# The first block's convolved projection with seven products of quarter sums, the weight sums made on GpSimd

## What is computed

```python
proj = h @ w_in[layer]                      # (256, 1024) @ (1024, 9304)
(..., qkv_b, ...) = jnp.split(proj, IN_SPLIT_IDX, axis=-1)     # qkv_b: 3072 columns
qkv_b = jax.nn.silu(causal_depthwise_conv(qkv_b, conv_w[layer]))   # 4 taps over the tokens
q_b, k_b, v_b = jnp.split(qkv_b, [1024, 2048], axis=-1)
q_b = l2_normalize(q_b.reshape(B, S, 8, 128))
k_b = l2_normalize(k_b.reshape(B, S, 8, 128))
```

## Time and profile before

| | us |
|---|---|
| median of 3 runs | 2429.8 (2429.56 to 2431.7) |
| the profiled execution's own time | 2429.32 |
| its span | 2427.4 |
| TensorE busy | 2369.2 (98%) |
| VectorE busy | 764.1 (31%) |
| ScalarE busy | 462.0 (19%) |
| GpSimd busy | 136.4 (6%) |
| mean granted TensorE clock | 0.992 of full speed |

### The profile page before, as it was taken

One profiled execution on the slowest core, in us unless ns is written; L12 is line 12 of the kernel. 1 busy time (PEld: TensorE's weight loads), 2 busy tenths in 40 slices (PEclk: granted clock), 3 DMA queues, 4 the chain that ended last, 5 costly groups with the idle time before them and its releaser, 6 DMA issues. The chain is left out here.

```text
span 2427.4 us, 51178 instructions
## 1 busy us (share of the span) xinstructions
PE 2369.2 (98%) x23267; PEld 1376.0 (57%) x23267; DVE 764.1 (31%) x1542; ACT 462.0 (19%) x793; POOL 136.4 (6%) x355
## 2 busy tenths in 40 slices
PE   9999999999999989999999899999999999999999
PEld 8755557856555666997455655435343534443444
DVE  3544623445633554663024532101010101101012
ACT  1531321432323542000015431000000000000001
POOL 4011000011000310000003100000000000000000
PEclk9999999999999999999999999999999999999999
DMA  7522334432335413445447128999999999999992
GB/s 244 166 88 72 120 122 139 145 105 71 108 116 142 158 54 126 166 162 177 142 129 192 55 91 330 397 405 373 384 391 383 372 395 396 398 378 392 389 370 97
DMA packets 194445, 542.54 MB, mean 224 GB/s; under 512 B 29200, under 2 KB 61360, under 8 KB 194224
## 3 DMA queue, kind: packets, MB, share of 16 engines
q1 hardware_dynamic: 180576, 536.82, 60.5%
q10 hardware_dynamic: 13344, 1.35, 0.4%
q0 software_dynamic: 304, 1.05, 0.1%
HBM read 538.12 MB, written 1.05 MB: 222 GB/s over the span
## 5 line engine op out<-in xcount | busy, mean ns | idle before, releaser
L405 PE MATMUL psum<-ring,hT 128*128 128x512 f32 (+3 forms) x1120 | 477.1, 575 | 6.1 <-ACT area L829 4.5
L2877 PE MATMUL psum<-ring,mix 128*32 128x448 f32 x4608 | 438.7, 539 | 0.2 <-DVE mix L3139 0.2
L405 PEld LDWEIGHTS psum<-ring,hT 128*128 128x128 f32 x1120 | 206.1, 190 | 206.1 <-issue 180.8
L2877 PEld LDWEIGHTS psum<-ring,mix 128*32 128x32 f32 x4608 | 149.1, 110 | 282.4 <-issue 280.6
L3128 DVE TENSOR_TENSOR area<-area,psum 128x1344 f32<-128x1344 f32 x16 | 24.6, 1535 | 457.6 <-PE psum L2877 457.6
L710 PE MATMUL psum<-hT,ring 128*128 128x256 f32 x768 | 166.4, 379 | 0.0
L710 PEld LDWEIGHTS psum<-hT,ring 128*128 128x128 f32 x768 | 146.1, 190 | 20.5 <-issue 1.0
L2890 PE MATMUL psum<-area 128*32 128x256 f32 x2688 | 148.2, 379 | 0.9 <-DVE area L3130 0.9
L2877 PE MATMUL psum<-area,mix 128*32 128x448 f32 x1536 | 147.3, 539 | 0.0
L2890 PE MATMUL psum<-ring,area 128*32 128x256 f32 x2688 | 146.5, 379 | 0.0
L2890 PEld LDWEIGHTS psum<-area 128*32 128x32 f32 x2688 | 86.7, 110 | 60.5 <-issue 2.9
(11 more groups left out here) (559 smaller groups left out, 2507.2 us busy)
## 6 DMA issues: line engine op xcount, KB each, us to landing
ring<-in_w_in_dram SPq DMA_DIRECT2D x88, 1024.0 KB, 5.1
ring<-in_moe_w_gate_dram SPq DMA_DIRECT2D x96, 896.0 KB, 7.0
ring<-in_moe_w_up_dram SPq DMA_DIRECT2D x96, 896.0 KB, 7.6
area<-in_moe_w_down_dram SPq DMA_DIRECT2D x112, 512.0 KB, 5.9
ring<-in_moe_w_down_dram SPq DMA_DIRECT2D x112, 512.0 KB, 6.3
area<-in_moe_w_gate_dram SPq DMA_DIRECT2D x32, 896.0 KB, 7.4
area<-in_moe_w_up_dram SPq DMA_DIRECT2D x32, 896.0 KB, 7.3
ring<-in_w_out_dram SPq DMA_DIRECT2D x16, 1024.0 KB, 5.1
```

The costliest lines, as they stand in the source:

```text
L405: last = nc.tensor.matmul(acc(g)[:, t, 0:d["n"]], lhs(kk, t), w[:, k, :], start=kk == 0, stop=kk == d["nk"] - 1)
L2877: last = nc.tensor.matmul(PS[32 * j:32 * j + 32, 3 * p + b, 0:PIECE].rearrange("p (m n) -> p m n", n=32), tokens(k, b), w[:, :, j, :], sta ...
```

## The change

Tile 0 stays as it was. Tiles 1 to 5 of each layer are computed by the seven-product form of Strassen and Winograd on one level: the weights are cut into four quarters (512 input rows by 256 columns), the input into four (512 channels by 128 tokens), and seven products of sums of quarters take the place of eight. A product is 8 matmuls of 128x128.

- `quarter_sums`: for each tile GpSimd makes four sums of 128x1024 from the tile's weights in the ring; all operands lie in SBUF. Two sets of buffers take turns, so the sums of tile i wait for the sixth product of tile i-2.
- `qkv_token_sums`: VectorE makes four sums of 128x512 of the input once per layer, behind the norm.
- `qkv_seven`: TensorE's products go round the four banks 0 to 3. The second product of a tile waits for GpSimd's sums; the fifth for ScalarE's copy of the first (`QKEPT`); the sixth and seventh for VectorE's reads of the second and third.
- `qkv_quarters`: VectorE joins the products by seven additions of 128x256, each with one input in PSUM and one in SBUF. They stand in VectorE's program ahead of the tile's convolution, and for tile 4 of the first layer ahead of the set-up.
- `proj1_act`: for tiles 1 to 5 ScalarE copies only the first product.
- Some semaphores are renamed into chains, so that there are enough of them.

```diff
+        def quarter_sums(s, eng, g, sums, name):
+            lo, hi = quarter_operands(g)
+            s1, s2, s3, s4 = sums
+            s.do(eng.tensor_tensor(s1, lo[:, :, IN1], hi[:, :, IN1], ALU.add))
+            s.do(eng.tensor_tensor(s2, s1, lo[:, :, IN0], ALU.subtract))
+            s.do(eng.tensor_tensor(s3, lo[:, :, IN0], lo[:, :, IN1], ALU.subtract))
+            s.after(eng.tensor_tensor(s4, hi[:, :, IN0], s2, ALU.subtract).then_inc(sem(name), 1), name)
+        def quarter_product(out, w, h):
+            for j in range(2):
+                for k in range(4):
+                    last = nc.tensor.matmul(out[:, j, :], w[:, k, j * P:(j + 1) * P], h[:, k, :], start=k == 0, stop=k == 3)
+            return last
+        def qkv_bank(i, place):
+            return PS[:, (2 + 7 * (i - 1) + place) % 4, 0:256].rearrange("p (j s) -> p j s", j=2)
+        def qkv_seven(pe, L, i):
...
+            order = ((lo[:, :, IN0], HT[:, 0:4, TOK0]), (s2, t2), (s1, t1), (s3, t3), (hi[:, :, IN0], HT[:, 4:8, TOK0]),
+                     (s4, HT[:, 4:8, TOK1]), (hi[:, :, IN1], t4))
+            gemm_begin(pe, g)
+            for h in range(2):
+                landed(pe, d["first"] + h)
+            for place, (w, h) in enumerate(order):
+                if place == 1:
+                    pe.wait_ge(sem("qkv_sums"), 5 * L + i)
+                if place == 2 and i == 1:
+                    pe.wait_ge(sem("gemm_out_act"), evacuated(group("qkv", L)[0])[1])
+                if place < 4:
+                    pe.wait_ge(sem("qkv_by_vector"), qkv_read(L, i - 1, 3 + place) if i > 1 else 31 * L + 1)
+                elif place == 4:
+                    pe.wait_ge(sem("gemm_out_act"), evacuated(g)[1])
+                else:
+                    pe.wait_ge(sem("qkv_by_vector"), qkv_read(L, i, place - 4))
+                quarter_product(qkv_bank(i, place), w, h).then_inc(sem("weights_used" if place > 4 else "qkv_product"), 1)
+        def qkv_pool(s, L):
+            if L:
+                x_half(s.eng, L, 1)
+            else:
+                s.eng.wait_ge(sem("param_cols_T"), 1)
+            for i in range(1, 6):
+                gs = group("qkv", L)
+                if i > 2:
+                    s.eng.wait_ge(sem("weights_used"), used(TILES[gs[i - 2]]["first"]))
+                for h in range(2):
+                    landed(s.eng, TILES[gs[i]]["first"] + h)
+                quarter_sums(s, nc.gpsimd, gs[i], QSUM[i % 2], "qkv_sums")
+        def qkv_token_sums(s):
+            t1, t2, t3, t4 = QTOK
+            s.do(nc.vector.tensor_tensor(t1, HT[:, 0:4, TOK1], HT[:, 0:4, TOK0], ALU.subtract))
...
+        def qkv_quarters(s, L, i):
...
+            first = 25 * L + 5 * (i - 1)
+            s.eng.wait_ge(sem("gemm_out_act"), evacuated(g)[1])
+            s.eng.wait_ge(sem("qkv_product"), first + 2)
+            told_read(add(QBOTH, qkv_bank(i, 1), QKEPT, ALU.add))
+            s.eng.wait_ge(sem("qkv_product"), first + 3)
+            told_read(add(QTHREE, qkv_bank(i, 2), QBOTH, ALU.add))
...
             for j, g in enumerate(group("qkv", L)):
-                s.eng.wait_ge(sem("weights_used"), used(TILES[g]["end"] - 1))
-                src = acc(g).rearrange("p b (j s) -> p (b j) s", j=2)
-                s.after(nc.scalar.activation(XC[:, 4 * j:4 * j + 4, 3:3 + S], src, ACT.Copy).then_inc(sem("gemm_out_act"), 1), "gemm_out_act")
+                if j:
+                    s.eng.wait_ge(sem("qkv_product"), 25 * L + 5 * (j - 1) + 1)
+                    if j > 1:
+                        s.eng.wait_ge(sem("qkv_by_vector"), qkv_read(L, j - 1, 4))
+                    dst, src = QKEPT, qkv_bank(j, 0)
...
+            qkv_token_sums(s)
             s.do(nc.vector.memset(XC[:, :, 0:3], 0.0))
...
             for j, g in enumerate(group("qkv", L)):
+                if j:
+                    qkv_quarters(s, L, j)
                 if L == 0 and j == 4:
                     setup_dve(s)
                     trig_tables(s, None)
...
             for L in range(DEPTH):
+                qkv_pool(s, L)
                 gdn_pool(s, L)
```

More of the change, by code:

```diff
@@ L670, in blocks_kernel @@
         XC = view(14512, CT * (S + 3)).rearrange("p (c s) -> p c s", c=CT)
+        QSUM = [[view(a, 1024).rearrange("p (k c) -> p k c", k=4) for a in (0, 1024, 3144, 4168)],
+                [v.rearrange("p (k c) -> p k c", k=4)
+                 for v in (mix_t[:, 0:1024], mix_t[:, 1024:2048], view(6288, 1024), view(7328, 1024))]]
+        QTOK = [view(a, 512).rearrange("p (k s) -> p k s", k=4) for a in (20728, 21240, 21752, 2048)]
+        QKEPT, QBOTH, QTHREE = [view(a, 256).rearrange("p (j s) -> p j s", j=2) for a in (22264, 5192, 5448)]
@@ new lines, in blocks_kernel, with quarter_operands @@
+        IN0, IN1, TOK0, TOK1 = slice(0, 256), slice(256, 512), slice(0, P), slice(P, S)
+        def quarter_operands(g):
+            return [half_view(TILES[g]["first"] + h, (4, 512)) for h in range(2)]
+        def quarter_sums(s, eng, g, sums, name):
[5 more added lines that the diff above has]
+            s.after(eng.tensor_tensor(s4, hi[:, :, IN0], s2, ALU.subtract).then_inc(sem(name), 1), name)
@@ new lines, in qkv_token_sums, with told_read @@
+        def qkv_token_sums(s):
+            t1, t2, t3, t4 = QTOK
+            s.do(nc.vector.tensor_tensor(t1, HT[:, 0:4, TOK1], HT[:, 0:4, TOK0], ALU.subtract))
+            s.do(nc.vector.tensor_tensor(t2, HT[:, 4:8, TOK1], t1, ALU.subtract))
+            s.do(nc.vector.tensor_tensor(t3, HT[:, 4:8, TOK1], HT[:, 0:4, TOK1], ALU.subtract))
+            s.after(nc.vector.tensor_tensor(t4, HT[:, 4:8, TOK0], t2, ALU.subtract).then_inc(sem("qkv_by_vector"), 1), "qkv_by_vector")
+        def qkv_quarters(s, L, i):
+            g = group("qkv", L)[i]
+            out = XC[:, 4 * i:4 * i + 4, 3:3 + S]
+            add = nc.vector.tensor_tensor
+            def told_read(ins):
+                s.after(ins.then_inc(sem("qkv_by_vector"), 1), "qkv_by_vector")
+            first = 25 * L + 5 * (i - 1)
[4 more added lines that the diff above has]
+            told_read(add(QTHREE, qkv_bank(i, 2), QBOTH, ALU.add))
+            s.eng.wait_ge(sem("qkv_product"), first + 4)
+            s.do(add(QBOTH, qkv_bank(i, 3), QBOTH, ALU.add))
+            told_read(add(out[:, 2:4, TOK1], qkv_bank(i, 3), QTHREE, ALU.add))
+            s.eng.wait_ge(sem("qkv_product"), first + 5)
+            told_read(add(out[:, 0:2, TOK0], qkv_bank(i, 4), QKEPT, ALU.add))
+            s.eng.wait_ge(sem("weights_used"), used(TILES[g]["first"]))
+            told_read(add(out[:, 0:2, TOK1], qkv_bank(i, 5), QTHREE, ALU.add))
+            s.eng.wait_ge(sem("weights_used"), used(TILES[g]["end"] - 1))
+            told_read(add(out[:, 2:4, TOK0], qkv_bank(i, 6), QBOTH, ALU.add))
@@ L700, in proj1_pe @@
             for i, g in enumerate(group("qkv", L)):
+                if i:
+                    qkv_seven(pe, L, i)
+                    if i == 3:
+                        sums(0)
+                    continue
                 d = TILES[g]
@@ L715, in proj1_pe @@
                             last.then_inc(sem("weights_used"), 1)
-                if i == 3:
-                    sums(0)
+            pe.wait_ge(sem("qkv_by_vector"), qkv_read(L, 5, 6))
             for _ in range(8):
@@ L766, in proj1_act @@
             for j, g in enumerate(group("qkv", L)):
-                s.eng.wait_ge(sem("weights_used"), used(TILES[g]["end"] - 1))
-                src = acc(g).rearrange("p b (j s) -> p (b j) s", j=2)
-                s.after(nc.scalar.activation(XC[:, 4 * j:4 * j + 4, 3:3 + S], src, ACT.Copy).then_inc(sem("gemm_out_act"), 1), "gemm_out_act")
+                if j:
[3 more added lines that the diff above has]
+                    dst, src = QKEPT, qkv_bank(j, 0)
+                else:
+                    s.eng.wait_ge(sem("weights_used"), used(TILES[g]["end"] - 1))
+                    dst, src = XC[:, 0:4, 3:3 + S], acc(g).rearrange("p b (j s) -> p (b j) s", j=2)
+                s.after(nc.scalar.activation(dst, src, ACT.Copy).then_inc(sem("gemm_out_act"), 1), "gemm_out_act")
                 if L == 0 and j < 4:
@@ L1371, in trig_tables @@
                     s.do(nc.vector.tensor_scalar(dst, dst, 3.1415925, -3.1415925, ALU.min, ALU.max))
-                s.after(nc.vector.tensor_copy(POSF, POSF).then_inc(sem("angles"), 1), "angles")
+                s.after(nc.vector.tensor_copy(POSF, POSF).then_inc(signal("angles"), 1), "angles")
             else:
                 s = s_act
-                s.eng.wait_ge(sem("angles"), 1)
+                s.eng.wait_ge(signal("angles"), reached("angles", 1))
                 s.do(nc.scalar.activation(SIN, SIN, ACT.Sin))
@@ L3531, in _ @@
             n = at_n = 0
[L3532 removed]
+            pe.wait_ge(signal("ident_ready"), reached("ident_ready", 1))
             keep_busy(3, 4)
```

31 lines of the change are left out of this document (20 added, 11 removed).

## The result

| | us |
|---|---|
| changed kernel, median of 4 runs | 2504.34 (2500.51 to 2506.15) |
| the kernel before, median of 4 runs beside it | 2430.75 (2429.56 to 2434.91) |
| ratio | 1.0298, 95% interval 1.0279 to 1.0316 |
| the profiled execution's own time, and its span | 2500.51, 2498.6 |

The account below looks back on a forecast made before the run. TensorE, busy 98% of the span, was taken to bound the kernel. 2429.3 + 32.5 (first layer) + 19.8 (second layer) + 8 (clock) = 2489.6, so 2490 us, with a 0.8 range of 2443 to 2510.

Parts of the forecast that it names:

- The products' saving: Tiles 1 to 5, both layers: 12.51 us a tile instead of 13.86, 13.5 us saved over ten tiles if nothing waits.
- A sum of 2.43 us: One 128x1024 weight sum on GpSimd alone takes 2.43 us, bounds 2.35 and 2.9; four take 10.0 us a tile.
- The first tile: First layer, tile 1: sums come behind GpSimd's set-up, so TensorE waits 13.8 us after the first product.
- Exclusive turns, one step to a sum: GpSimd's sums and VectorE's SBUF work take strict turns, one convolution step passing per sum; chance 0.65, own range 2474 to 2510.
- rival A: No long hold: a 1024-wide sum lets VectorE in between or hardly disturbs it; 2447, up to 2458 us; chance 0.27.
- The loop of 18.0 us: From one tile's sixth product to the next's: 18.0 us against 12.5, through sums, convolution, first join and semaphores.
- ScalarE at tile 5: Tile 5's fifth product waits for ScalarE's late copy: 11.3 us in the first layer; some 2.4 us late in the second.
- The norm: Second layer's start: eight GpSimd sums hold up VectorE's eight norm operations, so tile 0 ends 10.8 us later.
- The clock: After waits TensorE's clock falls to 1.2 GHz for 2.4, costing 8 us in all, bounds 0 to 16.
- Tile 2's wait: First layer: TensorE waits 6.5 us in tile 2, since its first sum runs before the convolution comes.
- B: Paid back, the faster side: TensorE's later waits absorb the delay; 2424 us; chance 0.03.
- C: The change doesn't do what it says: products need all eight banks, or sums come in time by chance; about 2430; chance 0.02.

Follow-up runs that it names:

- no_sums: Changed kernel without GpSimd's weight sums, the products taking plain weight quarters in their place: 2437.91 us, ratio 1.0028 to the kernel before.
- fills: Changed kernel with GpSimd's four sums replaced by fills with zero, which read nothing and keep GpSimd nearly as busy: 2456.61 us, ratio 1.0098 to the kernel before.
- copies: Changed kernel with each GpSimd sum replaced by two copies of one weight quarter, one SBUF operand read: 2481.12 us, ratio 1.0210 to the kernel before.

## Why the prediction was right, step by step

- **The products' saving** (12.51 us a tile): right. Without sums (no_sums) and where nothing waits the products follow each other every 1.79 us.
- **A sum of 2.43 us**: 2.34 to 2.50 in the first tile, most at 2.36; a little high.
- **The first tile** (13.8 us): 15.4. GpSimd's set-up ended at 41.0, not at 38.8. Of these 2.2 us, 1.25 lie in the one stretch that ran beside VectorE's token sums (21.40 to 24.27), new work of two SBUF operands; 0.2 is the later start of the whole, and 0.7 came at the end of the set-up, which now lies later beside tile 0's convolution. The stretch, of the kernel before and of the changed one:

```profile
21.43 1.56 POOL L3272 TENSOR_SCALAR_AFFINE_SELECT area<-area 128x128 f32<-128x128 f32 x4
```

```profile
21.66 2.81 POOL L3389 TENSOR_SCALAR_AFFINE_SELECT area<-area 128x128 f32<-128x128 f32 x4
```

  I had counted them as hidden under tile 0; they hide there from TensorE, not from GpSimd.
- **Exclusive turns, one step to a sum** (0.65): right, shown by the rows, by fills and copies, and by the second layer's scaled products, which are back at 2.77 us when GpSimd starts behind them. With fills the kernel took 2456.6, inside rival A's 2447 to 2458; A is wrong for sums. One point was too simple: the prediction reads the turns from steps with two SBUF inputs. The eight scaled products (13.91 us for 2.77) have two and bear it out, but the convolution's steps that were caught beside the sums have one (L1033).
- **The loop of 18.0 us**: the sixth products of tiles 2 and 3 start at 78.51 and 98.41, 19.9 us apart. With TensorE kept at full clock they are at 76.46 and 94.48, 18.0 apart (L773 is the first join there):

```profile
76.46 2.05 PE L696 MATMUL psum<-hT,area 128*128 128x128 f32 x16 [0.98 <-DVE area L773]
...
94.48 2.05 PE L696 MATMUL psum<-hT,area 128*128 128x128 f32 x16 [0.90 <-DVE area L773]
```

- **ScalarE at tile 5** (11.3 and 2.4): 11.5 and 2.1. **The norm** (10.8): from the norm's start to tile 1's first product it took 33.9 us (421.94 to 455.84) for 22.1 before, 11.8 more. Some 3 us of that are half clock, which the prediction had in another term, so the hold-up itself was about 2 us shorter than predicted.
- **The clock** (8 us, bounds 0 to 16): the term that was mis-sized. 19.6 us of delay show in the rows, and keeping TensorE busy gave back 12.1. I had laid the clock beside the stalls; it has to go into each chain, where a part lengthens it and a part is absorbed. The half-clock sixth product of tile 2 sits in the loop: it ends 1.8 us later, so GpSimd's next sums start 1.8 us later and the loop is 18.0 + 1.8. The seventh product behind it, 0.9 us late, only shortens the next wait: from the fifth product's end to the sixth's start tile 3 has 4.7 us in the changed kernel and 5.4 in the one kept busy. Tile 2's wait was simply put too high: 6.5 predicted, 5.5 with TensorE kept busy, 5.1 in the changed kernel.
- **The sum.** The profiled execution is 10.9 us above 2489.6: both stages together 42.9 + 24.7 - 60.3 = 7.3, the stretch between -2, the part behind the third norm 5.7, where the prediction had no term and whose cause is open. The 7.3 are two errors that partly cancel: the clock 11.6 more than the 8, TensorE's waits 37.6 + 20.7 = 58.3 for the predicted 39.3 + 26.5 = 65.8, and 3 us that no term here holds. So the closeness of 2490 to 2504 is in part luck. **B** (paid back) did not happen: 2 of 67.6 us came back. **C** did not either.

## What to carry to other kernels

GpSimd is no free helper beside a busy VectorE: each of its instructions that reads SBUF held off VectorE's SBUF work for its whole length, with one VectorE step passing for each. So the price of moving work there is the length of GpSimd's instructions (2.36 us a sum) wherever VectorE has SBUF work at the same time. Here VectorE made the same sums in half the time (1.225 us), in its idle stretch and in the gaps. Together with ScalarE's earlier copy and one tile left in the old form that turned 3.0% slower into 0.28% faster.

Ahead of a change that shortens the bounding engine's rows, list for every engine that now has to answer within the shorter time what stands in its queue ahead of the answer: ScalarE's tables and GpSimd's set-up alone cost more than the saving of 13.5 us. Where such answers are late, price the half clock inside the loop that the wait is part of.

## What the runs showed of the hardware that was not expected

- GpSimd's fill (no read) and VectorE's SBUF step of one operand also take turns: 2.81 us for four steps that take 1.14 alone, and the fill 1.10 for 0.95; VectorE's steps of two operands run beside fills at full speed (twelve in 5.09 us). Beside copies and sums both kinds wait.
- The seven joins, with one operand in PSUM and one in SBUF, keep 0.42 us beside sums and copies.
- A part of some 1490 us that the change does not touch differed by 3.1 us between two executions of the same kernel and by 8.3 between kernels, in step with the mean granted clock of its first stages (0.92 to 0.97 over 200 us), so a gain of 5 us elsewhere in this kernel can be hidden or doubled by it.
